# Attention of a four-layer decoder trunk: scores of two heads on 64 rows each, ones beside V, projection and attention interleaved

## The chip, the cores and the metric

The kernel runs on the 8 cores of one Trainium2 chip, one batch entry on each, with no exchange between cores. The metric is the device time of the slowest core in microseconds, as the median of the runs. A profile records one execution on all cores.

## What is computed

Four layers, each a token mixer and a gated feed-forward, with RMS norms around both. The attention of layers 0 and 3 is what the change touches.

```python
DILATED_CFG = ((128, 1), (512, 4), (2048, 16))   # (window, dilation) per head group
# 3 groups x 8 heads x 64 channels; x is (8, 2048, 1024), one batch entry per core
def dilated_group_attention(q, k, v, slopes, window, dilation):
    # query t attends keys t - j*dilation, j = 0..128: on each residue subsequence
    # a causal band, 128-query blocks against (previous, current) key blocks
    ...
    scores = jnp.einsum("brhnqc,brhnkc->brhnqk", qb, kb).astype(jnp.float32) * (HEAD_DIM ** -0.5)
    ...
    scores = jnp.where(valid, scores + bias[:, None], NEG_INF)      # ALiBi by true distance
    lse = jax.nn.logsumexp(scores, axis=-1)
    p = jnp.exp(scores - lse[..., None])
    o = jnp.einsum("brhnqk,brhnkc->brhnqc", p.astype(vb.dtype), vb)
    ...
def dilated_attention_mixer(x, w_qkv, w_o):
    ...
    wts = jax.nn.softmax(jnp.stack(lses, 0), axis=0)                # weights of the 3 groups
    merged = jnp.einsum("gbsh,gbshc->bshc", wts, jnp.stack(outs, 0).astype(jnp.float32))
    return merged.reshape(b, s, ATTN_WIDTH).astype(x.dtype) @ w_o

def reference(x, norm_g, ...):
    for i in range(4):      # mixer of layers 0..3: attention, short conv, pooling, attention
        x = x + rms_norm(mixer_i(rms_norm(x, norm_g[i, 0])), norm_g[i, 1])
        x = x + rms_norm(conv_ffn(rms_norm(x, norm_g[i, 2]), ...), norm_g[i, 3])
    return x
```

Since the groups are merged by their softmax denominators, the output of a head is the sum over the groups of exp(score) V, divided by the sum over the groups of exp(score). The kernel computes these two sums without a maximum.

## The kernel before

x, the residual stream, lies transposed in SBUF as fp32 (`X`, 8 channel chunks of 2048 tokens). Three weight buffers of 3072 columns (`WB`) are filled in turn from the POOL queue: `W.next` (L146), called where a block's work is built, issues loads up to two blocks ahead, and each load waits until the matmuls have read the block that it overwrites. Every operation goes through `P.op` (L37), so L137 is the line of nearly all of them in the profile. Each engine runs its own stream in the order in which the program builds it; `P.op` works out the semaphore waits from the ranges that an operation reads and writes.

`prenorm(l, j, tok0, ntiles)` (L326) goes by tiles of 512 tokens: ScalarE squares a chunk of X into one of two SB16 buffers, TensorE sums it by a ones matmul into bank 5 (eight times), ScalarE makes the reciprocal root with Ln and Exp (`stats_to_rs`, L274), and VectorE writes the normalised bf16 chunks into `XN` (the apply). Before layer 3 the end of the previous feed-forward has done this for tiles 0 and 1 (`pre_tiles` = 2); before layer 0 for none. That end (`ffn_down`, L486) also leaves VectorE 16 scalings and 16 adds for the residual (`res_add`).

`attention` (L572) runs in layers 0 and 3: prenorm of the tiles that are left, a memset of `BIG` from KAO to MO (8192 columns of zeros, L578), and then 12 stages, c in 0..3 (a pair of heads) times g in 0..2 (a group with dilation 1, 4 or 16). A stage does all its work before the next begins:

- P: Q and K of the pair for all 2048 tokens, 2 x 4 matmul groups of 8 with 512 columns, into five banks in turn (`ps_mm`, L220). ScalarE writes Q, residue by residue for g=1 and 2 (the view `p (r u) -> p u r`: PSUM is read in order, bf16 is written with a step of 512 or 128 elements). K goes out twice with zeros in the other head's rows, head A's 64 rows by ScalarE, head B's by VectorE, so that a full 128-row matmul gives one head's scores.
- V: 16 blocks of 128 keys, 8 matmuls of 128 columns each; again zero-padded per head, ScalarE and VectorE 256 columns each.
- A: 16 query blocks; `stage1(b)` (L637): 2 or 4 score matmuls (current block, previous block, per head), Exp by ScalarE to SB16, product with `MASK` by VectorE; `stage2` (L661), two blocks behind: 2 or 4 matmuls with V and as many with `ONESAB` for the denominators, both 128 columns wide, into banks 5, 6 and 7; then for g=0 a copy into `SCR` by ScalarE, for g=1 and 2 an add into `SCR` by VectorE with a token step of 4 or 16.

After the three groups of a pair, Ln and Exp(-x) of the denominators in SCR (ScalarE, 4 + 4 tiles of 512) and the product into `BIG` at MO (VectorE, 4). In layer 0 `build_mask` (L554) makes a stage's mask from 4 Exp and 4 products of 128 columns. The output projection (`proj_postnorm`, L330) follows; each of its tiles takes ScalarE twice, a copy and a square.

Of the kernel before, what the change touches and what calls it, by code (L numbers as in the profile page):

```python
# [6 lines left out]
F32 = mybir.dt.float32  # L7
# [158 lines left out]
def build_program(layers):  # L166
# [26 lines left out]
    with ExitStack() as st:  # L193
# [14 lines left out]
        ONESAB = sb("ONESAB", 256, BF16)  # L208
        HALO = sb("HALO", 88, F32)
        INVT = sb("INVT", 16, F32)  # L210
        PS = [st.enter_context(nc.psum_tensor("PS%d" % b, [128, 512], F32)) for b in range(8)]

        def construct(P, W):
# [39 lines left out]
            P.op("dve", I("memset", ONESAB[:, :], 0.0), writes=[("ONESAB", 0, 256)])  # L253
            P.op("dve", I("memset", ONESAB[:, 0:64], 1.0), writes=[("ONESAB", 0, 64)])
            P.op("dve", I("memset", ONESAB[:, 192:256], 1.0), writes=[("ONESAB", 192, 256)])

# [281 lines left out]
            def mask_setup():  # L538
                io_ap, io_rg = scr(9, 0, 128)
# [14 lines left out]
            def build_mask(g, c):  # L554
                vc, vc_rg = scr(8, 0, 128)
                vp, vp_rg = scr(8, 128, 128)
                dc, dc_rg = scr(8, 256, 128)
                dp, dp_rg = scr(8, 384, 128)
                for s_ in range(2):
                    h = 2 * c + s_  # L560
                    sd = float(2.0 ** (-8.0 * (g * 8 + h + 1) / 24.0)) * DIL[g]
                    mo = (g * 4 + c) * 512
                    for (d_ap, d_rg, v_ap, v_rg, co) in ((dc, dc_rg, vc, vc_rg, s_ * 128), (dp, dp_rg, vp, vp_rg, 256 + s_ * 128)):
                        t_ap, t_rg = scr(9, 128 + 128 * (mk[0] % 2), 128)
                        mk[0] += 1
                        P.op("act", I("activation", out=t_ap, in_=d_ap, func=AF.Exp, scale=-sd), reads=[d_rg], writes=[t_rg])
                        P.op("dve", I("tensor_tensor", out=MASK[:, mo + co:mo + co + 128], in0=t_ap, in1=v_ap, op=ALU.mult),
                             reads=[t_rg, v_rg], writes=[("MASK", mo + co, mo + co + 128)])

            QO, KAO, KBO, VO, MO = 0, 2048, 4096, 6144, 10240  # L570

            def attention(l, pre_tiles=0):  # L572
                prenorm(l, 0, 512 * pre_tiles, 4 - pre_tiles)
# [4 lines left out]
                P.op("dve", I("memset", BIG[:, KAO:MO], 0.0), writes=[("BIG", KAO, MO)])  # L578
                Vv = BIG[:, VO:MO].rearrange("p (b s c) -> p b s c", b=16, s=2)
                for c in range(4):  # L580
                    for g in range(3):
# [368 lines left out]
```

How the kernel before makes its waits and increments, by code:

```python
        def replay(e, name):  # L100
            for it in self.q[name]:
                if it[0] == "wait":
                    e.wait_ge(sems[it[1]], it[2])
                else:
                    ins = it[1](e)
                    if it[2] is not None:
                        ins.then_inc(sems[it[2]], it[3])
```

## Time and profile of the kernel before

| | us |
|---|---|
| median of 3 runs (3503.22 to 3503.83) | 3503.46 |
| profiled execution, slowest core (0): span, which is its own time | 3566.4 |
| profiled execution, all cores | 3498.5 to 3566.4 |
| core 0 busy: TensorE matmul | 3242.5 (91%) |
| core 0 busy: VectorE | 2357.5 (66%) |
| core 0 busy: ScalarE | 2266.2 (64%) |
| core 0 busy: GpSimd | 173.7 (5%) |

Layer 0's attention lies between 67 and 516 us on core 6, layer 3's between 2503 and 2941; the rest is short convolution, pooling and the four feed-forwards, which the change leaves alone. In the rows, PE is TensorE, PEld its weight load, ACT ScalarE, DVE VectorE, POOL GpSimd. An operation is named by tiles, out<-in. A matmul's duration runs from start to a modelled end, so that consecutive ones overlap: the pitch is the stretch divided by their count.

### The profile page before, as it was taken

The page shows a single profiled execution, that of the slowest core. Times are in us where ns is not written, and L with a number is a line of the kernel's source. Part 1 is how long each engine was busy: PE and PEld are TensorE (multiplying, and loading weights), DVE is VectorE, ACT ScalarE, POOL GpSimd, SP SyncE. Part 2 cuts the span into 40 slices and gives each one's busy share as a digit, 9 for nine tenths or more (in the row PEclk, how much of TensorE's full clock was granted, in tenths as well). Part 3 has the DMA queues.
Part 4 walks back from the last instruction along what each step waited for, and adds up shares of the span by engine and source line. Part 5 has one row for each costly group of instructions (what it writes and reads, how often), then busy time and mean ns, then how long its engine had stood idle before and what let it go on. Part 6 is the DMA issues. An engine that isn't in the chain of part 4 may idle for free. (4 is left out here: it accounts for less than half of the span.)

```text
span 3566.4 us, 58622 instructions; the slowest of 8 cores (3498.5 to 3566.4 us)
## 1 busy us (share of the span) xinstructions
PE 3242.5 (91%) x18761; PEld 1620.3 (45%) x19024; DVE 2357.5 (66%) x3736; ACT 2266.2 (64%) x4153; POOL 173.7 (5%) x333
## 2 busy tenths in 40 slices
PE   3988989999989999999987999998989888999996
PEld 1666653444434444444433444443566653443442
DVE  3555569929927669569476892983655668945852
ACT  3777778947832269649534794784677777944751
POOL 0000000000000010000000000000000000000000
PEclk9999999999999999999988999999999999988887
DMA  5111014443431164434414543343111104434332
GB/s 125 27 21 27 18 28 74 77 72 66 79 67 27 32 111 77 77 60 78 74 24 68 89 80 69 66 84 62 19 28 19 25 13 72 77 66 100 61 69 72
DMA packets 55018, 212.28 MB, mean 60 GB/s; under 512 B 6336, under 2 KB 6976, under 8 KB 54720
## 3 DMA queue, kind: packets, MB, share of 16 engines
q0 software_dynamic: 47232, 191.39, 30.8%
q1 hardware_dynamic: 5184, 12.94, 1.3%
q10 hardware_dynamic: 2304, 4.20, 0.4%
q8 instruction: 161, 2.64, 0.3%
q14 instruction: 137, 1.12, 0.1%
HBM read 391.47 MB, written 8.39 MB: 112 GB/s over the span
## 5 line engine op out<-in xcount | busy, mean ns | idle before, releaser
L137 PE MATMUL PS<-XN,WB 128*128 128x512 bf16 x8013 | 1817.9, 387 | 37.4 <-ACT SCR L137 18.4
L137 PEld LDWEIGHTS PS<-XN,WB 128*128 128x128 bf16 x8192 | 813.1, 99 | 1032.3 <-issue 187.8
L137 DVE SCALAR_TENSOR_TENSOR SCR<-SCR,DWV 128x512 f32<-128x512 f32 x1408 | 965.3, 744 | 39.9 <-ACT SCR L137 39.2
L137 ACT ACTIVATE SCR<-PS 128x512 f32<-128x512 f32 (+1 forms) x1120 | 633.4, 570 | 528.1 <-PE PS L137 473.3
L137 PE MATMUL PS<-BIG,WB 128*128 128x512 bf16 x3559 | 860.7, 392 | 26.0 <-DVE BIG L137 19.8
L137 PEld LDWEIGHTS PS<-BIG,WB 128*128 128x128 bf16 x3632 | 362.7, 100 | 473.1 <-issue 146.6
L137 ACT ACTIVATE SCR<-PS,DWV 128x512 f32<-128x512 f32 x704 | 487.2, 692 | 24.3 <-DVE X L137 12.4
L137 ACT ACTIVATE BIG<-PS 128x256 bf16<-128x256 f32 (+2 forms) x288 | 382.0, 1401 | 107.9 <-PE PS L137 88.1
L137 DVE SCALAR_TENSOR_TENSOR XN<-X,GV,SCR 128x512 bf16<-128x512 f32 x256 | 172.1, 744 | 384.7 <-ACT SCR L137 384.7
L137 ACT ACTIVATE SCR<-SCR 128x512 f32<-128x512 f32 (+2 forms) x704 | 327.5, 501 | 119.9 <-DVE SCR L137 90.1
L137 DVE CAST BIG<-PS 64x512 bf16<-64x512 f32 (+1 forms) x192 | 219.0, 1162 | 256.5 <-PE PS L137 166.0
L137 ACT ACTIVATE SB<-PS 128x512 bf16<-128x512 f32 (+1 forms) x640 | 339.9, 541 | 66.4 <-PE PS L137 37.2
L137 DVE SCALAR_TENSOR_TENSOR SCR<-SCR,GV 128x512 f32<-128x512 f32 x128 | 93.9, 744 | 346.7 <-ACT SCR L137 346.7
L137 PE MATMUL PS<-SB,ONES 128*128 128x512 bf16 x501 | 188.5, 418 | 139.1 <-ACT SB L137 135.3
L137 DVE TENSOR_TENSOR BIG<-SCR 128x512 bf16<-128x512 f32 x416 | 281.9, 684 | 29.1 <-ACT SCR L137 23.2
L137 ACT ACTIVATE XN<-PS 128x512 f32<-128x512 f32 x128 | 76.3, 596 | 254.5 <-PE PS L137 247.1
L137 DVE TENSOR_TENSOR SCR<-PS,SCR 128x256 f32<-128x256 f32 (+1 forms) x288 | 176.4, 617 | 41.1 <-ACT SCR L137 38.4
L137 PE MATMUL PS<-WB,XN 128*128 128x128 bf16 x3072 | 185.0, 221 | 3.7 <-ACT BIG L137 3.4
L137 PEld LDWEIGHTS PS<-WB,XN 128*128 128x128 bf16 x3072 | 182.3, 120 | 10.6 <-issue 5.0
L137 PE MATMUL PS<-SB,BIG 128*128 128x128 bf16 x1200 | 130.9, 220 | 61.1 <-DVE SB L137 48.0
L137 ACT ACTIVATE SB<-X 128x512 bf16<-128x512 f32 x256 | 150.8, 632 | 39.4 <-DVE X L137 21.2
L137 DVE TENSOR_TENSOR SB<-SB,MASK 128x512 bf16<-128x512 bf16 (+1 forms) x384 | 139.2, 364 | 54.1 <-ACT SB L137 32.3
(49 smaller groups left out, 1275.1 us busy)
## 6 DMA issues: line engine op xcount, KB each, us to landing
WB<-wup POOLq DMA_DIRECT2D x176, 512.0 KB, 6.1
WB<-wdn POOLq DMA_DIRECT2D x64, 704.0 KB, 7.3
WB<-wqkv POOLq DMA_DIRECT2D x24, 768.0 KB, 8.0
WB<-wo POOLq DMA_DIRECT2D x16, 512.0 KB, 6.2
WB<-cwout POOLq DMA_DIRECT2D x16, 512.0 KB, 5.9
WB<-pwout POOLq DMA_DIRECT2D x16, 512.0 KB, 6.1
WB<-cwin POOLq DMA_DIRECT2D x8, 768.0 KB, 7.7
X<-xT SPq DMA_DIRECT2D x8, 512.0 KB, 16.8
```

The costliest lines, as they stand in the source:

```text
L137: return lambda e: getattr(e, fn)(*a, **k)
```

## The change

Only `attention` and what it owns changes. (1) K is stored once, both heads in their own 64 partitions, and a score matmul uses one head's 64 rows; head s writes to its own bank, so that a slot of 2 query blocks (4 for g=2) fills two banks. A key block meets its own and the next query block in one matmul of 256 columns. (2) V of head A, 64 columns of ones and V of head B stand side by side in blocks of 192 columns; the left and the right 128 of them are stationary operands that give one head's values and its denominator together, heads in banks 4 and 5. The ones are written once per layer (`set_ones`). (3) Exp and mask product take both banks at once, the product in place; the result of 4 query blocks leaves both banks in one operation: a ScalarE copy for g=2, now the first group, a VectorE add for g=1 and 0. For g=0 Ln, Exp and product of that quarter follow at once, on half the partitions each. (4) Q, K and V of a stage lie in one of two sets in BIG, and the 12 units of the next stage's projection (8 for Q and K, 4 for V, through banks 6 and 7) are interleaved with the 9 slots (5 for g=2) of the present stage's attention. (5) Q and K are evicted through the view `p (u r) -> p r u`: PSUM is read with a step, bf16 is written in order; Q by ScalarE, K by VectorE. (6) The prenorm of the remaining tiles stands between the units of the first projection. (7) The masks of a head are built from 256 columns at once.

```diff
-        ONESAB = sb("ONESAB", 256, BF16)
-        PS = [st.enter_context(nc.psum_tensor("PS%d" % b, [128, 512], F32)) for b in range(8)]
+        PSALL = st.enter_context(nc.psum_tensor("PS", [128, 4096], F32))
+        PS = [PSALL[:, 512 * b:512 * b + 512] for b in range(8)]
...
-            QO, KAO, KBO, VO, MO = 0, 2048, 4096, 6144, 10240
+            SET, QO, KO, VO, MO = 7168, 0, 2048, 4096, 14336
+            VW = 192
...
-                prenorm(l, 0, 512 * pre_tiles, 4 - pre_tiles)
...
-                P.op("dve", I("memset", BIG[:, KAO:MO], 0.0), writes=[("BIG", KAO, MO)])
...
+                order = [(c, g) for c in range(4) for g in (2, 1, 0)]
+                pj = [0]
+                qkc = [0]
+                def ps_proj():
+                    b = 6 + pj[0] % 2
+                    pj[0] += 1
+                    return PS[b], "PS%d" % b
+                def set_ones():
+                    for st_ in range(2):
+                        vo = st_ * SET + VO
+                        P.op("dve", I("memset", BIG[:, vo:vo + 16 * VW].rearrange("p (b x) -> p b x", b=16)[:, :, 64:128], 1.0),
+                             writes=[("BIG", vo, vo + 16 * VW)])
...
+                        o = base + (KO if wh else QO)
+                        if Dl == 1:
+                            ov, iv, rg = BIG[:, o + 512 * tt:o + 512 * tt + 512], ps, ("BIG", o + 512 * tt, o + 512 * tt + 512)
+                        else:
+                            ov = BIG[:, o:o + S].rearrange("p (r u) -> p r u", r=Dl)[:, :, tt * nu:(tt + 1) * nu]
+                            iv = ps.rearrange("p (u r) -> p r u", r=Dl)
+                            rg = ("BIG", o, o + S)
+                        if wh == 0:
+                            P.op("act", I("activation", out=ov, in_=iv, func=AF.Copy), reads=[(psn, 0, 512)], writes=[rg])
+                        else:
+                            P.op("dve", I("tensor_copy", out=ov, in_=iv), reads=[(psn, 0, 512)], writes=[rg])
...
+                        vo = base + VO + b0 * VW
+                        ov = BIG[:, vo:vo + 4 * VW].rearrange("p (b s x) -> p b s x", b=4, s=3)[:, :, 0:3:2, :]
+                        iv = ps.rearrange("p (b s x) -> p b s x", b=4, s=2)
+                        P.op("act", I("activation", out=ov, in_=iv, func=AF.Copy), reads=[(psn, 0, 512)],
+                             writes=[("BIG", vo, vo + 4 * VW)])
+                    qs = [(lambda wh=wh, tt=tt: qk_unit(wh, tt)) for tt in range(4) for wh in range(2)]
+                    vs = [(lambda b0=b0: v_unit(b0)) for b0 in range(0, 16, 4)]
...
+                    def qk(j):
+                        qp = qkc[0] % 2
+                        eb = qkc[0] % 3
+                        qkc[0] += 1
+                        ebuf[j] = eb
...
+                                P.op("pe", I("matmul", PS[bk][:, co:co + n], lhsT=BIG[rows, ko:ko + 128], rhs=BIG[rows, qo:qo + n],
+                                             start=True, stop=True),
...
+                        P.op("act", I("activation", out=ev[:, :, 0:nc_], in_=pv_[:, :, 0:nc_], func=AF.Exp, scale=0.125),
...
+                        w_ = 128 if g == 2 else 256
+                        if nc_ == 512:
+                            ev4 = ev.rearrange("p s (b x) -> p s b x", x=w_)
+                            mul(ev4, mv[:, :, 0:w_].unsqueeze(2).broadcast_to([128, 2, 512 // w_, w_]))
+                        else:
+                            mul(ev[:, :, 0:256], mv)
+                            mul(ev[:, :, 256:384], mv[:, :, 0:128])
...
+                        P.op("pe", I("matmul", PS[4 + s_][:, dc:dc + n], lhsT=BIG[:, vo:vo + 128], rhs=SB16[:, po:po + n],
+                                     start=first, stop=last, skip_group_check=True),
...
+                    def pv(j):
+                        for b in range(per * j, per * j + per):
+                            i4 = b % 4
+                            prev = g != 2 and i4 == 0 and b % nb != 0
+                            for s_ in range(2):
+                                if prev:
+                                    pvmm(s_, b, (b - 1, 128), 128, 0, True, False, False)
+                                n = min(place[b][1], 128 * (4 - i4))
+                                pvmm(s_, b, (b, 0), n, 128 * i4, i4 == 0 and not prev, i4 == 3,
+                                     s_ == 1 and (i4 == 3 or b == per * j + per - 1))
+                            if i4 == 3:
+                                evict(b // 4)
+                    def evict(q):
+                        src = PSALL[:, 2048:3072].rearrange("p (s x) -> p s x", s=2)
+                        s_rg = [("PS4", 0, 512), ("PS5", 0, 512)]
+                        acc = SCR[:, 0:4096].rearrange("p (s t) -> p s t", s=2)
+                        if g == 2:
+                            dst = acc.rearrange("p s (u r) -> p s u r", r=16)[:, :, :, 4 * q:4 * q + 4]
+                            P.op("act", I("activation", out=dst, in_=src.rearrange("p s (r u) -> p s u r", r=4), func=AF.Copy),
+                                 reads=s_rg, writes=[("SCR", 0, 4096)])
+                            return
...
+                        P.op("dve", I("tensor_tensor", out=dst, in0=src, in1=dst, op=ALU.add), reads=s_rg + rg, writes=rg)
+                        if g == 0:
+                            a0, a1 = 512 * q, 512 * q + 512
+                            r_ap, r_rg = scr(10 + q % 2)
+                            lo_, hi_ = slice(0, 64), slice(64, 128)
+                            P.op("act", I("activation", out=r_ap[lo_, :], in_=SCR[hi_, a0:a1], func=AF.Ln), reads=[rg[0]], writes=[r_rg])
+                            P.op("act", I("activation", out=r_ap[hi_, :], in_=SCR[lo_, 2048 + a0:2048 + a1], func=AF.Ln),
+                                 reads=[rg[1]], writes=[r_rg])
+                            P.op("act", I("activation", out=r_ap, in_=r_ap, func=AF.Exp, scale=-1.0), reads=[r_rg], writes=[r_rg])
+                            for (rows, zo) in ((lo_, 0), (hi_, 2048)):
+                                P.op("dve", I("tensor_tensor", out=BIG[rows, mgo + a0:mgo + a1], in0=SCR[rows, zo + a0:zo + a1],
+                                              in1=r_ap[rows, :], op=ALU.mult),
+                                     reads=[rg[zo // 2048], r_rg], writes=[("BIG", mgo + a0, mgo + a1)])
+                    out = []
+                    for j in range(nst):
+                        def one(j=j):
+                            qk(j)
+                            if j:
+                                pv(j - 1)
+                        out.append(one)
+                    out.append(lambda: pv(nst - 1))
+                    return out
+
+                slots = []
+                for k in range(12):
+                    c, g = order[k]
+                    qs, vs = proj_units(k)
+                    if k == 0:
+                        for t in range(4):
+                            if t >= pre_tiles and t == 0:
+                                prenorm(l, 0, 0, 1)
+                            qs[2 * t]()
+                            if t + 1 < 4 and t + 1 >= pre_tiles:
+                                prenorm(l, 0, 512 * (t + 1), 1)
+                            qs[2 * t + 1]()
+                            if t == 1:
+                                set_ones()
                         if first_attn:
                             build_mask(g, c)
...
+                        for u in vs:
+                            u()
+                    else:
+                        units = qs + vs
+                        if first_attn:
+                            units.insert(3, lambda g=g, c=c: build_mask(g, c))
+                        n = len(slots)
+                        done = 0
+                        for ui, u in enumerate(units):
+                            u()
+                            while done < n and (done + 0.5) * len(units) / n <= ui + 1:
+                                slots[done]()
+                                done += 1
+                        while done < n:
+                            slots[done]()
+                            done += 1
+                    slots = attn_slots(k)
+                for f in slots:
+                    f()
```

## Rows read from the trace of the kernel before

**Rows 1.** Table of cores: span, mean granted TensorE clock.

```profile
core 0: 3566.4 us, clock 0.954
core 6: 3500.5 us, clock 0.974
```

**Rows 2.** Busy time by stretch, core 6, c=2: P, V, A (g=0), V, A (g=1), V, A (g=2).

```profile
core 6: us, PE busy (x) PEld busy (x) DVE busy (x) ACT busy (x) POOL busy (x), PEclk, DMA share, GB/s
296.00:309.70 13.70, 13.65 (x65) 6.24 (x66) 6.68 (x13) 9.12 (x19) 0.00 (x0) 1.00 0.01 2
309.60:316.90 7.30, 7.30 (x133) 7.30 (x132) 1.97 (x4) 1.74 (x4) 0.00 (x0) 1.00 0.01 2
316.80:331.40 14.60, 12.52 (x188) 10.62 (x187) 7.00 (x17) 13.35 (x32) 0.53 (x1) 1.00 0.31 57
345.00:353.00 8.00, 7.50 (x129) 7.19 (x127) 5.16 (x3) 7.72 (x5) 0.00 (x0) 1.00 0.01 2
353.60:368.20 14.60, 11.82 (x168) 9.69 (x170) 14.15 (x35) 9.39 (x22) 0.38 (x1) 1.00 0.31 56
381.80:390.10 8.30, 8.30 (x129) 8.09 (x127) 5.33 (x3) 8.02 (x5) 0.00 (x0) 1.00 0.01 2
390.60:403.30 12.70, 9.22 (x97) 6.74 (x99) 12.12 (x35) 6.62 (x20) 0.53 (x1) 0.87 0.35 65
```

**Rows 3.** Groups by shape, 316.8 to 331.4 (A, g=0): busy us, mean ns | idle before.

```profile
L137 ACT ACTIVATE SB<-PS 128x512 bf16<-128x512 f32 x15 | 8.9, 600 | 0.0
...
L137 ACT ACTIVATE SCR<-PS 128x256 f32<-128x256 f32 x15 | 5.7, 381 | 0.6 <-PE PS L137 0.4
```

**Rows 4.** Groups by shape, 353.6 to 368.2 (A, g=1).

```profile
L137 DVE TENSOR_TENSOR SCR<-PS,SCR 128x256 f32<-128x256 f32 x15 | 9.1, 611 | 0.0
...
L137 DVE TENSOR_TENSOR SB<-SB,MASK 128x512 bf16<-128x512 bf16 x12 | 4.9, 411 | 0.3 <-ACT SB L137 0.2
...
L137 DVE TENSOR_TENSOR SB<-SB,MASK 128x256 bf16<-128x256 bf16 x4 | 1.1, 277 | 0.0
```

**Rows 5.** Groups by shape, 331.4 to 345.1 (P, g=1): the Q eviction.

```profile
L137 ACT ACTIVATE BIG<-PS 128x512 bf16<-128x512 f32 x4 | 9.8, 2448 | 0.4
```

**Rows 6.** Groups by shape, 296.0 to 309.7 (P, g=0, and the previous pair's end).

```profile
L137 PE MATMUL PS<-XN,WB 128*128 128x512 bf16 x62 | 13.7, 379 | 0.1
...
L137 ACT ACTIVATE SCR<-SCR 128x512 f32<-128x512 f32 x8 | 4.3, 615 | 2.9 <-DVE SCR L137 2.9
...
L137 ACT ACTIVATE BIG<-PS 128x512 bf16<-128x512 f32 x4 | 2.4, 593 | 0.3
L137 DVE CAST BIG<-PS 64x512 bf16<-64x512 f32 x3 | 2.1, 694 | 2.8 <-PE PS L137 2.8
```

**Rows 7.** Groups by shape, 1088 to 1250 (layer 1): a contiguous fp32 VectorE operation from PSUM.

```profile
L137 DVE TENSOR_TENSOR SCR<-PS,SCR 128x512 f32<-128x512 f32 x32 | 22.1, 692 | 38.4 <-ACT SCR L137 38.4
```

**Rows 8.** Timeline, 510.6 to 517: start us, us, engine, operation [idle before <-releaser].

```profile
516.50 0.60 ACT L137 ACTIVATE SCR<-PS 128x512 f32<-128x512 f32 x1
```

**Rows 9.** Timeline of VectorE, 60 to 90 (start of layer 0).

```profile
61.54 5.39 DVE L137 SCALAR_TENSOR_TENSOR XN<-X,GV,SCR 128x512 bf16<-128x512 f32 x8 [15.46 <-ACT SCR L137]
69.14 5.39 DVE L137 SCALAR_TENSOR_TENSOR XN<-X,GV,SCR 128x512 bf16<-128x512 f32 x8 [2.21 <-ACT SCR L137]
...
76.72 6.88 DVE L137 MEMSET BIG<- 128x8192 bf16 x1 [1.65 <-issue]
```

**Rows 10.** Timeline of TensorE, 52 to 102 (start of layer 0).

```profile
85.04 7.94 PE L137 MATMUL PS<-XN,WB 128*128 128x512 bf16 x24 [7.64 <-ACT BIG L137]
92.81 7.31 PE L137 MATMUL PS<-WB,XN 128*128 128x128 bf16 x128
```

**Rows 11.** Timeline, 2501 to 2528 (start of layer 3): last residual to first scores.

```profile
2501.22 10.68 DVE L137 SCALAR_TENSOR_TENSOR XN<-X,GV,SCR 128x512 bf16<-128x512 f32 x16
...
2526.85 0.72 PE L137 MATMUL PS<-BIG 128*128 128x128 bf16 x10
```

**Rows 12.** Timeline, 2940 to 2942 (end of layer 3's attention).

```profile
2941.27 0.60 ACT L137 ACTIVATE SCR<-PS 128x512 f32<-128x512 f32 x1
```

**Rows 13.** The page's DMA issues: KB each, us from issue to landing.

```profile
WB<-wqkv POOLq DMA_DIRECT2D x24, 768.0 KB, 8.0
```

More of the change, by code:

```diff
@@ L554, in build_mask @@
             def build_mask(g, c):
[L555 to L558, printed above, removed]
+                v_ap, v_rg = scr(8, 0, 256)
+                d_ap, d_rg = scr(8, 256, 256)
                 for s_ in range(2):
@@ L561, in build_mask @@
                     sd = float(2.0 ** (-8.0 * (g * 8 + h + 1) / 24.0)) * DIL[g]
[L562 to L568, printed above, removed]
-            QO, KAO, KBO, VO, MO = 0, 2048, 4096, 6144, 10240
+                    mo = (g * 4 + c) * 512 + s_ * 256
+                    t_ap, t_rg = scr(9, 256 * (mk[0] % 2), 256)
+                    mk[0] += 1
+                    P.op("act", I("activation", out=t_ap, in_=d_ap, func=AF.Exp, scale=-sd), reads=[d_rg], writes=[t_rg])
+                    P.op("dve", I("tensor_tensor", out=MASK[:, mo:mo + 256], in0=t_ap, in1=v_ap, op=ALU.mult),
+                         reads=[t_rg, v_rg], writes=[("MASK", mo, mo + 256)])
+            SET, QO, KO, VO, MO = 7168, 0, 2048, 4096, 14336
+            VW = 192
             def attention(l, pre_tiles=0):
-                prenorm(l, 0, 512 * pre_tiles, 4 - pre_tiles)
                 first_attn = not masks_built[0]
@@ L688, in attention @@
-                        sts = [stage1(0), stage1(1)]
-                        for b in range(2, 16):
-                            sts.append(stage1(b))
-                            stage2(sts.pop(0))
-                        stage2(sts.pop(0))
-                        stage2(sts.pop(0))
-                    mgo = MO + c * S
-                    for q4 in range(4):
-                        a0, a1 = 512 * q4, 512 * q4 + 512
-                        P.op("act", I("activation", out=SCR[:, 2048 + a0:2048 + a1], in_=SCR[:, 2048 + a0:2048 + a1], func=AF.Ln),
-                             reads=[("SCR", 2048 + a0, 2048 + a1)], writes=[("SCR", 2048 + a0, 2048 + a1)])
@@ L699, in attention @@
-                    for q4 in range(4):
-                        a0, a1 = 512 * q4, 512 * q4 + 512
-                        P.op("act", I("activation", out=SCR[:, 2048 + a0:2048 + a1], in_=SCR[:, 2048 + a0:2048 + a1], func=AF.Exp, scale=-1.0),
-                             reads=[("SCR", 2048 + a0, 2048 + a1)], writes=[("SCR", 2048 + a0, 2048 + a1)])
-                    for q4 in range(4):
-                        a0, a1 = 512 * q4, 512 * q4 + 512
-                        P.op("dve", I("tensor_tensor", out=BIG[:, mgo + a0:mgo + a1], in0=SCR[:, a0:a1],
-                                      in1=SCR[:, 2048 + a0:2048 + a1], op=ALU.mult),
-                             reads=[("SCR", a0, a1), ("SCR", 2048 + a0, 2048 + a1)], writes=[("BIG", mgo + a0, mgo + a1)])
+                        for u in vs:
+                            u()
+                    else:
+                        units = qs + vs
[11 more added lines that the diff above has]
+                            done += 1
```

190 lines of the change are left out of this document (82 added, 108 removed).

## The prediction

> **What bounds the kernel now.** I read the table of cores first. Core 0 is the slowest at 3566.4 us with a mean granted clock of 0.954; core 6 ran at 0.974 and took 3500.5 us [rows 1]. The median of the runs, 3503.46, is 3.0 above core 6 and 63 below core 0, so the sum is made on core 6 with 3.0 added. The reader is to see that the page's core is not the one to subtract from.
>
> Then the busy time by stretch, for one head pair (c=2 of layer 0) [rows 2]. Each group g has a projection of Q and K (P), one of V (V) and an attention part (A). P is 13.7 us for 64 matmuls with PE busy to the end: 214 ns per 512 columns. V is 7.3, 8.0 and 8.3 us for 128 matmuls: 57 ns per 128 columns for g=0. A is 14.6, 14.6 and 12.7 us. Its 186, 168 and 96 matmuls of 128 columns would need 10.6, 9.6 and 5.5 us at 57 ns; PE looks 9 to 12 us busy only because each record includes the latency. So PE sets P and V and not A. In A of g=0 ScalarE is busy 13.35 of 14.6: 15 exponentials of 600 ns and 15 evictions of 381 ns [rows 3]. In A of g=1 VectorE is busy 14.15 of 14.6: adds of 611 ns into SCR beside 16 mask products [rows 4]. The opposite holds in P: VectorE is half idle. A pair costs 107.3 us (296.0 to 403.3), 42 of it A, and two layers have four pairs each.
>
> **The change, part by part.** All times per layer unless said.
>
> *Matmuls.* Scores: 62+56+32=150 of 128 columns per pair become 96, with K of one head on 64 rows; columns per head stay. With V and ones in one block, one matmul gives values and denominator: 300 of 128 columns become 102. A 256-column matmul, absent from the trace, lies between 57 and 214 ns; on the line between them, 109. Scores: g=0 30x109+2x57=3.4 us, g=1 24x109+8x57=3.1, g=2 32x57=1.8; PV the same within 0.1. A on PE is then 6.8, 6.2, 3.7 = 16.7 us per pair. PE's floor of a pair: 3x13.7+23.6+16.7=81.4 against 107.3.
>
> *Tiling of the array.* No row shows two matmuls on 64 rows each. Bounds: at best a pair of heads runs side by side and scores halve (-4.1 us per pair, 16 per layer); at worst the array empties at each of 160 changes between 64-row and 128-row matmuls (80 score groups) at latency less pitch, 379-214=165 ns [rows 2, 6]: +26. I take 0, between them. The Trainium skill (TensorEngine Tiling, Key Properties) says both: different tiles run in parallel, and changing the mode drains TensorE. By the first alone the time would be 32 us lower, by the second alone 53 higher; no run here shows it yet.
>
> *ScalarE and VectorE forms.* Exponentials now cover two banks, 1024 columns: 381 and 600 ns for 256 and 512 [rows 3] give 0.86 ns per column, so 1.04 us. Mask product, 277 and 411 ns [rows 4], on the same line: 0.68. V eviction is one of 512, 0.59, on ScalarE; contiguous Q 0.593, contiguous K now wholly on VectorE 0.694, Ln or Exp 0.615 [rows 6]. The add into SCR, contiguous 1024: 0.692 for 512 [rows 7] plus 512x1.04 = 1.22. Strided (g=1): 611 ns for 256 [rows 4] against 425 by that line, an excess of 0.73 ns per element, so 1.97.
> Q and K of g=1 and 2 now write contiguous bf16 but read PSUM at a step of 4 or 16 words; g=2 leaves by ScalarE reading at 128. No row reads PSUM with a step. Ends: 0 (Q 0.59) and what the bf16 write with a step costs now, 2448 against 593 ns, 3.6 ns per element [rows 5, 6]. I take the excess of the strided add, 0.73, the nearest row since it too touches a new 4-byte word each time: Q 0.97, K 1.07, g=2 eviction 1.04+0.75=1.79. The Trainium skill (Advanced Engine Details and Errata, Memory Cachelines) says PSUM lines hold two fp32 values and SBUF lines 16 bytes, with a penalty for each new line; it gives no price. By that rule every stepped PSUM read here pays (rival 2); the traced writes with a step agree that a penalty exists.
>
> *Interleaving.* Units of the next projection stand between attention slots. Three kinds of stage:
> - g=1 projection over g=2 attention: PE 13.7+8.0+3.6=25.3. ScalarE 4x0.97+4x0.59+4x1.04+4x1.79=17.6: hidden. 25.3.
> - g=0 over g=1: PE 13.7+7.3+6.2=27.2. But banks 4 and 5 are single. The add that frees them comes on VectorE behind the mask product of the newest slot: after the score matmuls 0.2+1.04+0.68+1.97 plus handovers = 4.3 us, while PE has 0.45 (PV), one unit 1.7 and the next scores 0.45 = 2.6 to do. Twice a stage the next slot is only one unit away: 1.7 us lost each. 30.7.
> - g=2 over g=0: PE 13.7+8.3+6.8=28.8. Now the chain per quarter is exponential 1.04, mask 0.68, add 1.22, two Ln and an Exp on ScalarE 1.85, next exponential 1.04, with handovers 6.0 us; 1.33 Q evictions (1.3) and in part K's (0.5) sit in it. Over 2.67 quarters beside Q/K units 7.8 each, 1.33 beside V units 6.8 each, plus the lead-in of 4: 34. This is the stage where a wait takes the place of the old one: the two Ln head ScalarE's queue waiting for VectorE's add, and behind them stand the Q eviction and the next exponential, for which PE waits.
>
> Sum of the eleven stages: 4x25.3+4x30.7+3x34=326.
>
> *Tail.* The last g=0 attention has no projection beside it: 2 slots of lead and four quarters of 6.0, so ScalarE is free for the output projection about 26 us after the last V. Before, A plus the final Ln, Exp and product end at 516.5 and 2941.3, the first evictions of the output projection [rows 8, 12]. It needs ScalarE twice per tile, so this is the point to compare.
>
> *Start.* Layer 0: a memset of 6.88 us holds VectorE [rows 9], PE stands 7.64 us and V ends at 100.1 [rows 10]. Now units for token tiles 0 and 1 run while x is still arriving, and two memsets of 1024 replace one of 8192. But the squares of tile 3 come on ScalarE behind the Q eviction of tile 2, which waits for the apply of tile 2: tile 2 is applied by 66.9, unit and Q eviction end 68.3, squares, Ln and Exp take 7.6 from apply to apply [rows 9], the apply 5.4, the last Q/K unit 1.9, V 8.3, and 1.4 for matmuls at 1.2 GHz after the idle: 93. Gain 7. Layer 3: V ended 2526.9, with the squares of tile 3 done while VectorE was at the residual, which it leaves at 2501.2 [rows 11]. Now: K eviction and apply to 2507.7, unit and Q eviction to 2509.3, then the same 7.6, 5.4, 1.9, 8.3 and 1.4: 2534. Loss 7.
>
> *At nothing.* Weight loads stay one per stage on the POOL queue, 8.0 us to land [rows 13], against a stage of 25 and a ring of three; with less than 8 us of cover they would show. ONESAB memsets fall before the x load. Mask building halves its instructions.
>
> **Sum.** Layer 0: 416.4 (100.1 to 516.5) - 352 (326+26) + 7 = 71.4. Layer 3: 414.4 (2526.9 to 2941.3) - 352 - 7 = 55.4. 3500.5-126.8+3.0=**3376.7 us**.
>
> **Rivals.**
> 1. PE-bound throughout: ScalarE and VectorE run ahead, no wait for a bank. Stages 25.3, 27.2, 28.8 give 296, 30 less per layer: 3317; with overlapped pairs 3285. For: ScalarE's total is under PE's in each stage. Against: banks 4 and 5 are single, and the Ln follow an add in a FIFO. 0.13.
> 2. Reading PSUM with a step costs 2 to 3.5 ns per element over the plain read. At 2.0 ScalarE's work in the first stage reaches 25.3 and the third stage 37: 3395. From there each further ns adds 6.1 us per first stage (6,144 such elements) and 2.5 per third: at 2.8 it is 3450. For: the bf16 write with a step does pay 3.6 today. Against: the fp32 adds with a step pay 0.73. 0.08.
> 3. The other side: the same reads at 3.6 ns or more. Place: BIG<-PS and SCR<-PS on ScalarE in the g=1 projection stage. At 3.6 the stage has 4x2.45+2.4+4.1+4x4.7=35.1 us of ScalarE, the third 41: 386 for the eleven, 3502. That is the point from which the change loses; at 5 it is 44 and 45 us, 3590. 0.05.
> 4. The drain of the array at each mode change and no overlap: 160x0.165 per layer, 3429. 0.08.
> 5. It doesn't do what it says: PE's in-order stream puts projection units behind attention that waits, and every slot serializes. Then stages are P+V+A as now, and only fewer instructions remain: A 10 instead of 14 us, some 3450. 0.03.
>
> Besides, a denser PE may be granted less clock, as core 0 of this profile was (0.954): up to +60, counted in the range of each.
>
> **How the numbers follow.** Forecast 0.63. Its bounds are 3330 and 3425: an excess of 0 on the stepped reads makes it 3365, half of the two stalls gone takes 30 more, and the tiling ends are -32 and +53. The range reaches down to rival 1's first figure and up past rival 4 to the middle of rival 2, 3315 to 3450. It leaves out 3285, the dear half of rival 2 and rival 3, and what I haven't thought of: 0.2. A measurement of this kernel tells 0.2%, 7 us, from nothing. Faster: all but rival 3, 0.95; of rival 3, 0.01 is no change and 0.04 slower.
>
> **What would show it.** Stages of 25, 31 and 34 us on PE in the profile after; PE waiting for SCR adds before PV; ScalarE idle until VectorE's SCR before Ln; BIG<-PS of 128x512 near 0.97 us; V of layer 3 ending later than 2527. Wrong if BIG<-PS stays near 2.4, if score matmuls of the two heads start together and PE's stages fall under 28, or if gaps of 0.16 us stand at each mode change.

## The result and the profile after

The changed kernel took 3384.4 us where the kernel before took 3503.5: a ratio of 0.966 (95% interval 0.964 to 0.968). In some executions pairs of cores are granted less clock and take longer, so the time given for a kernel is that of its shortest execution, and spans and stages are of cores that were not held back. The forecast was 3376.7, 7.7 too low; the range held the time.

The cores of the profiled execution agree, so core 6 can be set against core 6 [rows 1]: 3500.5 to 3382.7, a gain of 117.8 where the sum had 126.8.

```profile
core 0: 3379.9 us, clock 0.966
...
core 6: 3382.7 us, clock 0.966
```

A head pair was P, V and A in turn [rows 2]. Now a stage is one projection with the previous group's attention between its units. There are three kinds of stage: the first is the projection of g=1 over the attention of g=2, the second g=0 over g=1, the third g=2 over g=0. Busy time by stretch, core 6: two lines of layer 0 (second and third kind), then three of layer 3 (first, second, third). Columns as in rows 2.

```profile
209.70:241.70 32.00, 27.26 (x253) 16.66 (x256) 14.43 (x21) 12.24 (x19) 0.53 (x1) 1.00 0.14 26
241.70:276.10 34.40, 29.11 (x259) 17.93 (x262) 18.35 (x25) 17.77 (x28) 0.53 (x1) 1.00 0.13 24
2648.10:2673.30 25.20, 24.51 (x254) 15.81 (x256) 8.13 (x11) 13.82 (x19) 0.53 (x1) 1.00 0.19 33
2673.30:2704.10 30.80, 27.32 (x255) 16.67 (x257) 13.85 (x19) 11.96 (x17) 0.53 (x1) 1.00 0.16 27
2704.10:2736.80 32.70, 29.18 (x261) 18.03 (x263) 17.59 (x23) 17.35 (x26) 0.53 (x1) 1.00 0.14 25
```

In layer 3 a pair costs 88.7 us, against 107.3 for a pair of layer 0 before [rows 2] and 91.7 now (25.3, 32.0 and 34.4), and the clock stands at 1.00 throughout. PE is busy 81.0 of 88.7; ScalarE and VectorE reach 55% of a stage at most. The first stage is PE-bound (24.5 busy of 25.2). The second has 3.5 us of idle PE, the third 3.5. In layer 0 the second is longer by 1.2 and the third by 1.7.

The groups by shape in layer 3's attention, 2472.3 to 2792.4 (busy us, mean ns | idle before):

```profile
L137 ACT ACTIVATE SB<-PS 128x1024 bf16<-128x1024 f32 x53 | 53.8, 1020 | 39.6 <-PE PS L137 39.6
L137 ACT ACTIVATE BIG<-PS 128x512 bf16<-128x512 f32 x88 | 52.3, 594 | 92.1 <-PE PS L137 92.1
L137 DVE TENSOR_TENSOR SB<-SB,MASK 128x1024 bf16<-128x1024 bf16 x53 | 36.7, 692 | 76.7 <-ACT SB L137 76.4
L137 DVE CAST BIG<-PS 128x512 bf16<-128x512 f32 x44 | 30.4, 690 | 58.7 <-PE PS L137 58.2
L137 ACT ACTIVATE SCR<-PS 128x1024 f32<-128x1024 f32 x16 | 16.5, 1029 | 0.0
```

The second line is the Q and V evictions of all three groups, the fourth K's. Q and K of g=1 and 2, 28 of the 88 and of the 44, read PSUM at a step of 4 or 16 words. The means are those of contiguous evictions, 594 and 690 ns against 593 and 694 [rows 6], where writing with a step cost 2448 [rows 5]. The last line reads at a step of 128: 1029 ns.

PE's waits in the same stretch (total, times, longest):

```profile
PE PS L137 <- DVE SCR L137: 17.1, 15, 1.6
PE PS L137 <- DVE SB L137: 5.1, 3, 1.7
PE PS L137 <- ACT BIG L137: 1.5, 4, 0.6
```

The first line is PE waiting for the add that frees banks 4 and 5.

### The profile page after: what moved, and what is told of

Same layout as the page of the kernel before. It is cut to its first block and busy times, and to the rows that moved or that the text cites. A ratio compares the mean times of both kernels' runs of the same rounds, so it can differ in the third digit from the quotient of the medians.

```text
span 3382.7 us, 50942 instructions; the slowest of 8 cores (3378.9 to 3382.7 us)
## 1 busy us (share of the span) xinstructions
PE 3061.0 (90%) x16734; PEld 1469.5 (43%) x17008; DVE 2162.9 (64%) x3271; ACT 1971.8 (58%) x3745; POOL 173.7 (5%) x333
## 5 line engine op out<-in xcount | busy, mean ns | idle before, releaser
L137 ACT ACTIVATE SCR<-PS 128x512 f32<-128x512 f32 (+1 forms) x1024 | 616.7, 607 | 459.0 <-PE PS L137 413.7
L137 PE MATMUL PS<-BIG,WB 128*128 128x512 bf16 x3559 | 830.6, 382 | 17.8 <-DVE BIG L137 12.0
L137 ACT ACTIVATE SCR<-SCR 128x512 f32<-128x512 f32 (+3 forms) x712 | 350.6, 518 | 147.6 <-DVE SCR L137 134.4
L137 DVE TENSOR_TENSOR BIG<-SCR 128x512 bf16<-128x512 f32 (+1 forms) x448 | 305.7, 684 | 82.6 <-ACT SCR L137 73.5
L137 ACT ACTIVATE SB<-PS 128x512 bf16<-128x512 f32 (+2 forms) x416 | 305.6, 737 | 78.5 <-PE PS L137 76.8
L137 ACT ACTIVATE BIG<-PS 128x512 bf16<-128x512 f32 x192 | 114.2, 595 | 284.4 <-PE PS L137 284.4
L137 DVE TENSOR_TENSOR SB<-SB,MASK 128x1024 bf16<-128x1024 bf16 (+2 forms) x200 | 111.1, 558 | 186.9 <-ACT SB L137 181.3
L137 DVE TENSOR_TENSOR SCR<-PS,SCR 128x1024 f32<-128x1024 f32 (+1 forms) x96 | 124.9, 1301 | 77.9 <-PE PS L137 41.0
L137 PE MATMUL PS<-SB,BIG 128*128 128x128 bf16 (+1 forms) x816 | 98.7, 255 | 80.7 <-DVE SCR L137 41.9
L137 POOL DMA_DIRECT2D WB<-wup x176 | 92.9, 528 | 1205.4 <-PE PS L137 1179.4
```

The lines of the kernel that those rows point to most:

```text
L137: return lambda e: getattr(e, fn)(*a, **k)
```

## The experiments

All are edits of the changed kernel, and stage lengths are read as PE's from the first matmul of one projection to that of the next. With nothing edited, layer 3 has 25.0 to 25.3, 30.8 and 32.4 to 32.7, layer 0 25.3, 32.0 and 34.4 (the first stage of each layer takes 24.5, and one third stage of layer 0 takes 36.0, at a granted clock of 0.95), and the tail, last V to first output projection on PE, is 26 to 27.

**Nothing changed, beside other runs.**

> The changed kernel itself once more, as the base of the runs beside it: 3384, stages of 25.3, 30.8 and 32.4 us in layer 3 and 1.5 to 2 more in the two longer ones of layer 0.

The slowest core took 3414.0; six of the eight had spans of 3380.0 to 3383.8, and the stages were those above. So spans compare across these runs to some 3 us, and stage lengths to 0.3, but for that one third stage of layer 0.

**The interleave undone.**

```
 for ui, u in enumerate(units):
     u()
-    while done < n and (done + 0.5) * len(units) / n <= ui + 1:
-        slots[done]()
-        done += 1
```

> The changed kernel (3384.4 us) with its interleaving alone undone: all twelve projection units of a stage first, then all attention slots. Everything else of the change stays. Theory (attention is bound by its chains and the projection fills the gaps): the attention of a pair alone runs at the pace of its chain, 8 slots of g=2 at about 2.6 us, 8 or so of g=1 at about 2.7, four quarters of 6.0 us and a lead of 2 at g=0, together 55 to 60 us beside 64.7 of projections, 120 to 125 per pair against the 92 that the stages take now: some 3600 to 3660 us, slower even than the kernel before. Rival A (rival 5 of the prediction: the gain is that of fewer instructions): attention alone takes 10 us a stage, 95 per pair, and the time stays within 30 us of 3385 or goes to 3450 at most. Rival B (PE-bound): same.

3655.6 us, ratio to the kernel before 1.037 (1.029 to 1.044). Three stages of layer 0, core 6 (g=2, g=1 and g=0 projection, each followed by its predecessor's attention):

```profile
293.80:342.40 48.60, 33.63 (x260) 19.69 (x262) 18.55 (x26) 18.25 (x27) 0.53 (x1) 0.75 0.09 17
342.40:375.40 33.00, 27.55 (x254) 17.47 (x256) 8.79 (x13) 14.05 (x21) 0.53 (x1) 0.86 0.15 25
375.40:417.70 42.30, 31.16 (x255) 18.18 (x257) 14.55 (x22) 13.37 (x19) 0.53 (x1) 0.78 0.11 20
```

123.9 us a pair, in the 120 to 125 expected of chains. Rival 5 falls: the change without its interleaving loses 3.7% to the kernel before. That each 1024-column step is a longer chain with nothing under it would explain this, but is argued from the forecast and not tested by itself. Part of the 270 us between this and the changed kernel is clock: its mean is 0.75 to 0.86 of 2.4 GHz in these stages, where PE stood idle between slots, against 1.00. PE is busy 92.3 us in the three against 80.8 in the same stages interleaved, so at most some 11 of the 32 us that such a pair loses are clock. The projection at 342.4, behind the longest attention, took PE 15.9 us instead of 13.7 [rows 2].

**Scores on 128 rows.** `lhsT=BIG[rows, ...], rhs=BIG[rows, ...]` becomes `BIG[:, ...]`.

> The changed kernel with the score matmuls on all 128 rows instead of 64: no change of the array's tiling and no two matmuls side by side. Left out: the separation of the two heads (each score is the sum over both heads). Same number of matmuls and columns. Theory of the prediction (tiling costs and gives nothing net): 3385, within 5. If pairs of 64-row matmuls overlap: four of 256 columns take 0.33 us to the next group in the trace against 0.44 on the line between 57 and 214 ns, 0.1 us for each of about 60 groups a layer, up to 12 us slower; with full overlap up to 32 slower. If the array drains at 160 changes a layer at 0.165 us: up to 53 us faster.

3388.7 us, spans of 3380 to 3388; stages of 25.0, 30.9 and 32.5 to 32.8. TensorE in the first, PE-bound stage: a projection unit, scores, PV (the matmuls with V) and the next unit. The 128-row kernel first, then the changed one:

```profile
2663.88 3.40 PE L137 MATMUL PS<-XN,WB 128*128 128x512 bf16 x15
2667.12 0.61 PE L137 MATMUL PS<-BIG 128*128 128x128 bf16 x8
2667.56 0.61 PE L137 MATMUL PS<-SB,BIG 128*128 128x128 bf16 x8
2668.01 3.62 PE L137 MATMUL PS<-XN,WB 128*128 128x512 bf16 x16
```

```profile
2657.07 3.40 PE L137 MATMUL PS<-XN,WB 128*128 128x512 bf16 x15
2660.41 0.40 PE L137 MATMUL PS<-BIG 64*128 64x128 bf16 x8
2660.74 0.62 PE L137 MATMUL PS<-SB,BIG 128*128 128x128 bf16 x8
2661.19 3.62 PE L137 MATMUL PS<-XN,WB 128*128 128x512 bf16 x16
```

Start to start: the unit takes 3.24 us ahead of 128-row scores and 3.34 ahead of 64-row ones; eight scores take 0.44 and 0.33; PV 0.45 in both. The cycle is 4.13 and 4.12. What lies under the 0.11 is seen when the window is narrowed to 0.01 us, at the first score (128 rows, then 64):

```profile
2667.12 0.22 PE L137 MATMUL PS<-BIG 128*128 128x128 bf16 x1
```

```profile
2660.41 0.23 PE L137 MATMUL PS<-BIG 64*128 64x128 bf16 x2
```

On 64 rows the two heads' matmuls start together. By the single records of layer 3's attention the second starts 2 to 4 ns behind the first in all of 176 pairs, and the next pair of 128 columns some 53 to 56 ns later, where on 128 rows every single matmul takes 56. So the scores run fully side by side, and four pairs save 0.22 us. From the last 512-column matmul to the first score it is 312 ns instead of 216, and from the last pair to PV 149 instead of 56: each change costs some 0.095, in both directions. The Trainium skill (TensorEngine Tiling, Key Properties) says that different tiles run in parallel and that changing the mode needs a drain. The trace agrees with the first, and shows a price at each change: 0.095 where the prediction's upper end had 0.165. Gain 0.22 and price 0.19 a group nearly cancel. The 0 taken between the ends stands, and rival 4 falls.

**Write with a step instead of read.**

```
-ov = BIG[:, o:o + S].rearrange("p (r u) -> p r u", r=Dl)[:, :, tt * nu:(tt + 1) * nu]
-iv = ps.rearrange("p (u r) -> p r u", r=Dl)
+ov = BIG[:, o:o + S].rearrange("p (r u) -> p u r", r=Dl)[:, tt * nu:(tt + 1) * nu, :]
+iv = ps.rearrange("p (u r) -> p u r", r=Dl)
```

> The changed kernel with the views of the Q and K evictions of g=1 and 2 as they were before: read in order, written as bf16 at a step of 4 or 16, 2.45 us each instead of 0.60 and 0.69. The mechanism of rivals 2 and 3 at half its size. Theory (ScalarE's order counts where it stands in the chain of a quarter): in the g=1 projection stage ScalarE has 4x2.45+4x0.6+4x1.02+4x1.03=20.4 us of 25.3, hidden; in the g=2 projection stage over g=0 attention 1.33 evictions stand in a quarter, 2.5 us more for each of 2.67 quarters, 6.6 us per stage, six such stages: 40 us slower, 3425. Rival (totals count, not order): ScalarE's 28 us of the 32.4 stage are under it: within 7 us of 3385. Rival (every us of it counts, also in the first stage): 4x1.85 per stage, 14 stages, 100 us slower.

(The innermost step of the write is 512 or 128 elements, as in the kernel before; 4 and 16 are the steps of the changed kernel's reads.) 3498.2 us, spans of 3484 to 3497, some 110 slower: nearly all of the gain. My theory's 40 missed by a factor of nearly three; the number of the last rival, 100, came nearest. On core 3 third stages are 40.4 us in layer 3 (one 42.2) and 41.8 in layer 0, some 8 more. Unforeseen, first stages are 28.5 to 28.8 (+3.5) and 31.2 to 32.8 (+6 to 7.5), and the first projections, which no stage counts, take most of the last 20 us: the one of layer 0 ends 14 later. Waits of PE in one first stage of layer 0, core 3:

```profile
PE PS L137 <- DVE BIG L137: 3.0, 2, 2.8
PE PS L137 <- ACT BIG L137: 2.9, 2, 2.2
```

I had counted ScalarE's total, 21.8 of 32.8 us. But a projection has two PSUM banks, one for Q and one for K in turn, so PE stands at the next unit when an eviction of 2.45 us stands behind Ln and Exp (2.07 for three), an output copy (1.03) or a mask product (0.69). This is the price of rivals 2 and 3, on a side that the changed kernel doesn't use, and it works by the wait for a bank, where those rivals and I had added up ScalarE's total. With Q and K alone at that price it gives 3498, where I had put rival 3, g=2 eviction included, at 3502 (its own stages add up to 3497).

**Masks early.** All twelve `build_mask` calls go ahead of the first projection.

> The changed kernel with all twelve masks of layer 0 built ahead of the attention's first projection, where VectorE and POOL wait for x, instead of one among the units of each stage. Theory (the mask building in the stages is what makes the eleven stages of layer 0 12.8 us longer than those of layer 3, 332.9 against 320.1): 11 to 13 us faster, 3372, with the stages of layer 0 at 30.7 and 32.4 as in layer 3. Rival (the stages of layer 0 are longer for another reason, such as the arrival of weights or the placing of buffers): same, or slower by what the masks push into the start.

3374.7 us, 10 less. Layer 0, core 6:

```profile
208.80:239.60 30.80, 27.33 (x255) 16.67 (x257) 13.84 (x19) 11.98 (x17) 0.53 (x1) 1.00 0.15 27
239.60:272.30 32.70, 29.11 (x261) 17.99 (x263) 17.58 (x23) 17.34 (x26) 0.53 (x1) 1.00 0.14 26
```

The stages are those of layer 3: over eleven of them 12.6 us less, and the start is 2.6 later. 1.6 of the 12.6 are what the one third stage at a clock of 0.95 takes more than the other two; here all have 1.00. The kernel and the trace show where the rest comes from. The changed kernel puts the mask building of a stage into the list of projection units (`units.insert(3, ...)`), as a thirteenth unit without any TensorE work, and spaces the slots over thirteen. So the slots before and after it follow each other with no projection between them. Layer 0, timeline (start us, us, engine, operation [idle before]):

```profile
215.48 0.61 PE L137 MATMUL PS<-SB,BIG 128*128 128x256 bf16 x4
215.86 0.81 ACT L137 ACTIVATE SB<-PS 128x768 bf16<-128x768 f32 x1
...
216.02 0.39 PE L137 MATMUL PS<-BIG 64*128 64x256 bf16 x4
216.55 0.72 ACT L137 ACTIVATE SCR<-SCR 128x256 f32<-128x256 f32 x2
216.77 0.82 DVE L137 TENSOR_TENSOR SB<-SB,MASK 128x512 bf16<-128x512 bf16 x2 [2.38 <-ACT SB L137]
217.17 1.02 ACT L137 ACTIVATE SB<-PS 128x1024 bf16<-128x1024 f32 x1
217.51 0.75 DVE L137 TENSOR_TENSOR MASK<-SCR 128x256 bf16<-128x256 f32 x2
217.74 0.49 PE L137 MATMUL PS<-SB,BIG 128*128 128x256 bf16 x4 [1.33 <-DVE SB L137]
```

PE goes from PV (215.48) to the next scores (216.02) and at once needs the product that starts at 216.77. The exponential before it (215.86) and that product run ahead of the mask's own operations (216.55 and 217.51), so these don't cause the 1.33 us; the missing unit does. The same wait stands in every second and third stage of layer 0, and in the third PE then waits 2.2 us for a K eviction. PE's waits in layer 0's eleven stages (93.3 to 423), changed kernel:

```profile
PE PS L137 <- DVE SB L137: 10.8, 10, 1.6
PE PS L137 <- DVE BIG L137: 6.6, 3, 2.2
```

With the masks early the first is 5.4 in 3 waits and the second isn't there. The edit takes away both the mask's operations and their place among the units. That the place is most of the cost is read from the trace; a run with the masks in place, but not counted as a unit, wasn't made.

**Add ahead of the mask product (g=1).** In the slot, scores and exponential, then PV and its add, then the mask product, which `qk` now hands back for g=1:

```
-qk(j)
+late = qk(j)
 if j:
     pv(j - 1)
+if late is not None:
+    late()
```

> The changed kernel with one order of VectorE changed, in the attention of g=1 alone: the add that frees banks 4 and 5 stands ahead of the newest slot's mask product instead of behind it. Theory (the two stalls of 1.6 us in a stage of the g=0 projection over g=1 attention come from that order): the add of 2.0 us then starts when PV ends and the mask product 0.69 follows it; PE has a unit of 1.7 and scores of 0.35 to do meanwhile, so a stall of some 0.65 us is left of 1.6, the stage goes from 30.8 to 28.8 us, and eight such stages give 8 to 16 us, 3370 to 3376. Rival (PE waits there for the add whatever stands ahead of it, or for another thing): stage of 30.8, time the same within 2.

3374.1 us, 10.3 less; stages 29.2 instead of 30.8 in layer 3, 30.4 to 30.7 instead of 32.0 in layer 0. Timeline, the changed kernel first, then this one:

```profile
2506.69 0.69 DVE L137 TENSOR_TENSOR SB<-SB,MASK 128x1024 bf16<-128x1024 bf16 x1 [0.81 <-ACT SB L137]
2507.30 1.97 DVE L137 TENSOR_TENSOR SCR<-PS,SCR 128x1024 f32<-128x1024 f32 x1
...
2509.41 0.60 PE L137 MATMUL PS<-SB,BIG 128*128 128x256 bf16 x4 [1.57 <-DVE SCR L137]
```

```profile
2501.93 2.01 DVE L137 TENSOR_TENSOR SCR<-PS,SCR 128x1024 f32<-128x1024 f32 x1
...
2503.83 0.70 DVE L137 TENSOR_TENSOR SB<-SB,MASK 128x1024 bf16<-128x1024 bf16 x1
...
2504.68 0.60 PE L137 MATMUL PS<-SB,BIG 128*128 128x256 bf16 x4 [0.86 <-DVE SB L137]
```

The stall is where the prediction put it, twice a stage, of 1.6 us (1.7 forecast). With the add first 0.86 is left (0.65 expected), now on the mask product.

**Ln and Exp one slot later (g=0).** Two Ln, Exp and products are issued after the next exponential.

> The changed kernel with the two Ln, the Exp and the products of a quarter of g=0 issued one slot later, behind the next exponential, instead of ahead of it in ScalarE's queue. Theory (the two Ln at the head of ScalarE's queue, waiting for VectorE's add, are what makes the g=2 projection stage over g=0 attention 32.4 us instead of PE's 28.8, and the tail's quarters 6.7): stage of 29.5 us, 2.9 less in each of six; in the two tails three quarters of 1.8 less each; together 28 us, 3357. Rival (that stage is bound by the chain exponential, mask product, add or by the Q and K evictions): 32 us and a time within 5 of 3384.

3376.1 us, 8 less, not 28. Third stages of layer 3 are 31.1 (-1.4, not -2.9), those of layer 0 even 35.0 (+0.6), where the masks still stand among the units; the tails are 20.2 and 20.9 instead of 26 to 27, as expected. ScalarE's wait for VectorE's add in layer 3, the changed kernel and then this one:

```profile
ACT SCR L137 <- DVE SCR L137: 34.7, 16, 4.1
```

```profile
ACT SCR L137 <- DVE SCR L137: 7.3, 6, 1.7
```

The wait that I had named is real and goes; in the stage PE work is what comes next (29.0 busy of 31.1), so little of it was on the path. In the tail nothing covers it.

**Layer 3's tiles 2 and 3 normalized first.**

> The changed kernel with the squares, statistics and applies of token tiles 2 and 3 of layer 3's first projection issued ahead of its first units, as the kernel before had them; layer 0 is left as it is. Theory (the squares of tile 3 behind the Q eviction of tile 2 cost layer 3's start 5.7 us): V of the first stage ends 5 to 6 us earlier against the end of the feed-forward before it, 3378. Rival (the start there is bound by VectorE leaving the residual, whichever order follows): same within 1 us, or later by what the first units wait.

3384.0 us. From the feed-forward's last statistics matmul before it to the end of the first V: 47.2 us in the kernel before, 51.9 to 52.7 in the changed one, 51.3 here. So 1 us, not 5.7: my cause for the loss falls. TensorE in the changed kernel, then here:

```profile
2441.78 6.39 PE L137 MATMUL PS<-XN,WB 128*128 128x512 bf16 x16 [9.31 <-DVE BIG L137]
```

```profile
2443.36 7.41 PE L137 MATMUL PS<-XN,WB 128*128 128x512 bf16 x24
2453.35 10.48 PE L137 MATMUL PS<-XN,WB 128*128 128x512 bf16 x40 [2.58 <-DVE BIG L137]
```

Both waits are for a K eviction on VectorE, first behind the residual, here behind sixteen applies that end at 2452.6.

**K evictions of that projection on ScalarE.** `if wh == 0:` becomes `if wh == 0 or (k == 0 and pre_tiles == 2):`, on top of the last edit.

> The changed kernel with two edits in layer 3's first projection: squares, statistics and applies of tiles 2 and 3 ahead of its first units (as in the run that gained 1 us of the 5.7), and the K evictions of that projection on ScalarE instead of VectorE. Theory (the loss at layer 3's start is PE waiting for one of only two projection banks, whose K eviction stands on VectorE behind the applies or the residual): no wait at 2451, the last Q/K unit ends 7.4 us after the last apply as in the kernel before instead of 11.3, V of the first stage ends 49 us after the last statistics of the feed-forward instead of 52.7 (before 47.1), 3379 us. Rival (a slower TensorE clock after the long idle sets it): 52 us or more, 3383.

```profile
2443.22 15.93 PE L137 MATMUL PS<-XN,WB 128*128 128x512 bf16 x64
2458.99 8.15 PE L137 MATMUL PS<-WB,XN 128*128 128x128 bf16 x128
```

No gap, and 46.8 us from statistics to V: the loss is gone, and more than expected (49). The time by itself says little: 3388.7, on a chip where the kernel before took 3510.5 instead of 3503.5; four cores had spans of 3376 to 3380.

**The gains together.** Masks early, add first, Ln late, tiles 2 and 3 first.

> The three changes that gained, together (masks built early, add ahead of the mask product at g=1, Ln and Exp of a quarter one slot later), with layer 3's tiles 2 and 3 normalized first. If they add up: stages of 25.0, 29.2 and 31.1 us in both layers, tails of 20.5, start of layer 0 2.7 later: layer 0 gains 25, layer 3 17, 3342 us. If they share a cause: 3355 or more.

Stages of 25.0, 29.2 and 31.1 to 31.3 in both layers, tails of 20.2 to 20.6. 3354.6 us, 0.956 of the kernel before (0.953 to 0.959) on a chip where that one took 3510.5. Cores 0 to 3 had spans of 3340 to 3346, those of the changed kernel 3380 to 3382. The four by themselves gave 10, 10, 8 and less than 1. They add up, and to some 8 more: Ln late costs layer 0's third stages 0.6 beside the masks, and without them they come down to 31.3 with the others.

**The add first at g=0 too.**

> The same with the add ahead of the newest mask product at g=0 as well. Theory (the quarter's chain in the g=2 projection stage is still exponential, mask product, add, and VectorE frees banks 4 and 5 0.7 us earlier per quarter): stages of 30 instead of 31.1 and quarters of the tail 0.7 shorter, 8 to 10 us under the run without it. Rival (the mask product, now behind an add of 1.2 us, holds PV and so the next quarter up): stages of 31.5 to 32, slower by 2 to 6.

3405.1 us, 50 slower than without it; third stages of 38 instead of 31.2, tails of 26. The rival's sign, at some ten times its price. In the third stage from 2526.7 to 2564.4, core 3 (VectorE, then PE):

```profile
2541.52 1.48 DVE L137 TENSOR_TENSOR BIG<-SCR 64x512 bf16<-64x512 f32 x2 [3.66 <-ACT SCR L137]
2543.03 0.69 DVE L137 TENSOR_TENSOR SB<-SB,MASK 128x1024 bf16<-128x1024 bf16 x1
...
2543.87 0.71 PE L137 MATMUL PS<-SB,BIG 128*128 128x256 bf16 x4 [3.15 <-DVE SB L137]
```

The held-back mask product now stands behind the products of the quarter before, and VectorE is idle 3.66 us before these, waiting for ScalarE's Exp; PE waits 3.15 for the mask product, three such waits and 7.1 us in this stage. The order that helped at g=1 puts a waiting instruction ahead of what PE needs once the later Ln stand beside it. Whether it helps at g=0 without them wasn't tried.

**All that gained.** The combination with K on ScalarE.

> The three changes that gained (masks early, add ahead of the mask product at g=1, Ln and Exp of a quarter one slot later) and the K evictions of layer 3's first projection on ScalarE, with its tiles 2 and 3 normalized first. If the four add up: stages of 25.0, 29.2 and 31.2 us in both layers, tails of 20.5, V of layer 3's first stage 46.8 us after the last statistics before it; against the changed kernel's 3384: layer 0 25 us, layer 3 22 us less, 3338 us on a chip where the kernel before takes 3503, 0.953 of it. If the last gives nothing beside the others: 3342, 0.954.

3342.7 us against 3503.5 on the same chip, 0.954. That is 42 us under the changed kernel and 161 under the one before. It rests on one execution, with spans of 3336 to 3341; in four of the five others some cores reach it, at 3331 to 3339.

## Why the prediction was right, and where not

**Base and sum.** Core 6 was the right base; the slowest core lies 1.7 above it now, not 3.0, so 9.0 too much gain and 1.3 too much added make the 7.7. Layer 0 gained 60.5 us to its first output eviction (516.50 to 456.04) where the sum had 71.4; layer 3 gained 58.2 more, against 55.4.

**PE's work.** 81.0 us busy a pair measured, 81.4 summed; the records' ends are modelled, so the better witness is the PE-bound first stage (25.3 forecast). The 109 ns for 256 columns came out: four of PV take 0.43 us. The tiling's 0 held by luck: it was taken between two ends with no row for either, and both were there, a full overlap worth 16 us a layer and 160 changes at 0.095, which cost 15.

**Stages.** First: 25.3 forecast, 25.0 to 25.3. Second: 30.7 forecast, 30.8 in layer 3; its stall is in the trace and shrinks with the add first. Third: 34 forecast, 32.4 to 32.7 in layer 3. The chain exists, but its share on the path was put too high: I let 2.67 quarters wait 7.8 us each, while taking Ln and Exp out gave back only 1.4 a stage.

**Stepped reads.** The mis-sized term: 0.73 ns per element taken, 0 measured. With 0 the forecast would have been 3365, further off: the error hid another. The add that gave the price reads PSUM in order; its step is in SCR, on SBUF, and so it was no row for a stepped PSUM read. The Trainium skill (Advanced Engine Details and Errata, Memory Cachelines) says that a non-contiguous PSUM pattern slows matmuls significantly; I carried that over to ScalarE's and VectorE's reads, and these show nothing of it (594 against 593 ns, 690 against 694). Rivals 2 and 3 had nothing to stand on, though their price, put on the writes, costs 110 us.

**Masks.** The step that failed: "Mask building halves its instructions", booked at nothing. It costs 12.6 us over layer 0's stages, 10 net of what it takes at the start when done early. Before, layer 0's attention was only 2 us longer than layer 3's (416.4 and 414.4 in the sum). I priced its instructions and not its place: as a unit without TensorE work it leaves two slots with nothing between them, and nearly all of the extra waits follow from there.

**Tail.** 26 forecast to ScalarE's first output eviction, 30 measured (2792.4 to 2822.64). The four Ln start 6.75 to 6.86 us apart, not 6.0, the first 7.9 after V. 4 us in each layer.

**Starts.** Layer 0: V ends at 93.2 and the forecast was 93. Layer 3: loss of 5.5, forecast 7, for a wrong reason. Not the squares behind the Q eviction, but K evictions on VectorE behind residual and applies, with two banks to the projection, as the last two runs at that start show.

**How the misses add.** Against the sum: eleven stages of layer 3 took 320.1 us and not 326, and layer 0's would without masks, -12; masks +13; tails +8; layer 3's start -1.5. That is 7.5 of the 9.0 by which the gain was overrated: the sum was closer than its terms, because they cancel, and that is luck. One rival's price doesn't follow from its own terms: 4 us less in each of 24 stages puts rival 5 at 3407, not 3450, and the run without interleaving took 3655.6. Rival 1 (PE-bound, 3317) is the direction in which the last version lies, at 3342.7, with 2 us still idle in each of the longer stages.

## What to carry to other kernels

When two phases are interleaved, space the slots of one by the TensorE work of the other: a unit without such work (mask building here) leaves a hole, in which TensorE waited 1.3 to 1.6 us each time. Judge an eviction by the number of PSUM banks before its reader and by what stands ahead of it in its engine's queue, not by the engine's total. After each reordering look again at which waiting instruction is at the head of a queue; an order that helps in one stage can cost more in the next.

## What the runs showed of the hardware

Reading PSUM with a step of 4, 16 or 128 fp32 words costs ScalarE nothing that shows (594 and 1029 ns for 512 and 1024 columns), the first two VectorE nothing (690), while writing bf16 to SBUF with a step of 512 or 128 elements costs 2.45 us for 512. Put the step on the read. Matmuls of 128 columns on the two halves of the array start 3 ns apart, a pair every 53 to 56 ns (on 128 rows one matmul every 56), and each change between 128 and 64 rows, either way, costs some 0.095 us. With PE idle between slots the mean granted clock of a stage was 0.75 to 0.86, interleaved 1.00.
